# Order of the matmuls inside a contraction step of gate and up: four of 512 columns, then four of 256

## The reference, cut to what matters

```python
def swiglu_ffn(h, w_gate_up, w_down):
    gate, up = jnp.split(h @ w_gate_up, 2, axis=-1)
    return (jax.nn.silu(gate) * up) @ w_down
...
    for layer in range(DEPTH):
        h = h + 0.5 * swiglu_ffn(rms_norm(h, ffn1_norm[layer]), ffn1_w_gate_up[layer], ffn1_w_down[layer])
        ...
        h = h + 0.5 * swiglu_ffn(rms_norm(h, ffn2_norm[layer]), ffn2_w_gate_up[layer], ffn2_w_down[layer])
    return rms_norm(h, final_norm)
```

## Time and profile before

| what | value |
|---|---|
| median of 3 runs | 1030.55 us |
| the runs | 1030.55, 1028.49, 1701.71 us |
| the profiled execution, its own time | 1029.14 us |
| its span, first to last instruction | 1027.4 us |
| TensorE busy | 1016.9 us (99%), 5790 matmuls |
| loads of its stationary operand | 881.5 us (86%), 5790 |
| VectorE busy | 675.4 us (66%) |
| ScalarE busy | 569.1 us (55%) |
| granted TensorE clock, mean | 0.999 |

### The profile page before, as it was taken

The page is one execution under the profiler, slowest core; times in us unless marked ns, Lnnn a source line. Parts: engine busy times, 40 slices in busy tenths (PEclk is TensorE's granted clock), DMA queues, the critical chain, the costliest instruction groups (busy, mean ns, idle before and its releaser), DMA issues.

```text
span 1027.4 us, 15453 instructions
## 1 busy us (share of the span) xinstructions
PE 1016.9 (99%) x5790; PEld 881.5 (86%) x5790; DVE 675.4 (66%) x1005; ACT 569.1 (55%) x907; POOL 60.3 (6%) x120
## 2 busy tenths in 40 slices
PE   8999999999999999999999999999999999999997
PEld 7888888887888888888888888999999988888886
DVE  5766765576566776635766764688597666776733
ACT  7645543457565654536545543577567655554532
POOL 0000000110000000000000000404205100000000
PEclk9999999999999999999999999999999999999999
DMA  9666465343346555563665465343242347556521
GB/s 322 214 208 200 163 245 201 138 165 109 99 130 228 172 186 216 212 199 102 196 213 191 166 243 205 118 155 123 83 144 83 124 144 231 179 176 219 213 87 41
DMA packets 124308, 175.81 MB, mean 171 GB/s; under 512 B 7360, under 2 KB 97760, under 8 KB 124256
## 3 DMA queue, kind: packets, MB, share of 16 engines
q1 hardware_dynamic: 121552, 172.77, 49.5%
q10 hardware_dynamic: 2704, 2.33, 0.7%
HBM read 174.02 MB, written 1.06 MB: 170 GB/s over the span
## 4 chain that ended last, share of the span: by engine, by line
PE 97%; DVE 1%; ACT 1%; DMA 1%; issue 0%; SPq 0%; ACTq 0%; DVEq 0%
PE bank L1761 29%; PE bank L1691 15%; PE bank L1693 15%; PE bank L1692 14%; PE bank L1763 14%; PE bank L2085 2%; PE bank L2079 2%; PE bank L1988 1%; PE bank L1712 1%; PE bank L1923 1%; PE bank L1954 1%; PE bank L1853 1%; DMA w_raw<-in_ffn_w_gate_up 1%; DVE x_sb L1184 0%; PE bank L2182 0%
## 5 line engine op out<-in xcount | busy, mean ns | idle before, releaser
L1761 PE MATMUL bank<-xT,w_hi 128*128 128x512 f32 x1280 | 444.9, 394 | 0.0
L1147 DVE TENSOR_TENSOR w_lo<-w_raw,w_hi 128x2048 fp32r<-128x2048 f32 x152 | 347.4, 2290 | 105.7 <-ACT w_hi L727 105.0
L727 ACT ACTIVATE w_hi<-w_raw 128x2048 fp32r<-128x2048 f32 x153 | 294.0, 1930 | 118.0 <-PE bank L1693 118.0
L1763 PE MATMUL bank<-xT,w_lo 128*128 128x256 f32 x1280 | 354.8, 277 | 0.0
L1761 PEld LDWEIGHTS bank<-xT,w_hi 128*128 128x128 f32 x1280 | 240.0, 188 | 55.7
L1763 PEld LDWEIGHTS bank<-xT,w_lo 128*128 128x128 f32 x1280 | 240.4, 188 | 0.1
L1691 PE MATMUL bank<-w_hi,hT_hi 128*128 128x512 f32 x352 | 137.5, 391 | 0.0
L1693 PE MATMUL bank<-w_hi,hT_lo 128*128 128x512 f32 x352 | 137.0, 389 | 0.0
L1692 PE MATMUL bank<-w_lo,hT_hi 128*128 128x512 f32 x352 | 137.0, 389 | 0.0
L793 ACT ACTIVATE silu_g<-bank 128x256 f32<-128x256 f32 x80 | 26.4, 382 | 175.4 <-PE bank L1763 175.4
L1234 DVE TENSOR_TENSOR silu_g<-bank,silu_g 128x256 f32<-128x256 f32 x80 | 30.2, 419 | 119.5 <-ACT silu_g L793 119.5
(11 more groups left out here) (312 smaller groups left out, 1218.7 us busy)
## 6 DMA issues: line engine op xcount, KB each, us to landing
w_raw<-in_ffn_w_gate_up SPq DMA_DIRECT2D x170, 512.0 KB, 4.6
w_raw<-in_ffn_w_down SPq DMA_DIRECT2D x88, 512.0 KB, 4.0
w_raw<-in_gdn_w_in SPq DMA_DIRECT2D x32, 512.0 KB, 4.4
w_raw<-in_attn_w_in SPq DMA_DIRECT2D x12, 512.0 KB, 4.1
w_raw<-in_attn_w_out SPq DMA_DIRECT2D x8, 512.0 KB, 3.7
w_raw<-in_gdn_w_out SPq DMA_DIRECT2D x8, 512.0 KB, 3.6
w_raw<-in_ffn_w_gate_up SPq DMA_DIRECT2D x12, 256.0 KB, 6.1
x_sb<-in_x SPq DMA_DIRECT2D x4, 256.0 KB, 5.4
```

The source lines that it names most:

```text
L727: act.activation(w_hi[u0 % RING][:], w_raw[u0 % RING][:], ACT.Copy).then_inc(hi_ready, 1)
L1147: dve.tensor_tensor(w_lo[u0 % RING][:], w_raw[u0 % RING][:], w_hi[u0 % RING][:].bitcast(F32), ALU.subtract).then_inc(split_ready, 1)
L1761: pe.matmul(banks[m][:], w[0], xT[:, kt, :, :].rearrange("p s n -> p (s n)"), start=(kt == 0), stop=False, skip_group_check=True)
L1763: z = pe.matmul(banks[m][:, SEQ:2 * SEQ], w[1], xT_hi[:, kt, :], start=False, stop=(kt == KT - 1), skip_group_check=True)
```

## The change

Within a contraction step all four matmuls of line 1761 are issued first, banks 0 to 3, and then the four with `w_lo`, banks 0 to 3. The number of matmuls and of loads, their operands, the waits and the place of `unit_done` (behind the last matmul of a unit, with `w_lo` on bank 3) stay. Each bank still gets its `w_hi` matmul before its `w_lo` matmul of the step. The second kind stands at line 1765 of the new file.

```diff
@@ -1760,6 +1760,8 @@
                             w = ring(u0, slice(q * BANK + m * P, q * BANK + (m + 1) * P))
                             pe.matmul(banks[m][:], w[0], xT[:, kt, :, :].rearrange("p s n -> p (s n)"),
                                       start=(kt == 0), stop=False, skip_group_check=True)
+                        for m in range(4):
+                            w = ring(u0, slice(q * BANK + m * P, q * BANK + (m + 1) * P))
                             z = pe.matmul(banks[m][:, SEQ:2 * SEQ], w[1], xT_hi[:, kt, :], start=False,
                                           stop=(kt == KT - 1), skip_group_check=True)
                     z.then_inc(unit_done, 1)
```

## The result

| | before | after |
|---|---|---|
| median | 1028.61 us (six runs, the three shown above among them) | 1033.32 us (six runs, 1032.77 to 1033.53) |
| ratio | 1 | 1.0042, 95% interval 1.0029 to 1.0055 |
| span of the profiled execution | 1027.4 us | 1031.6 us |

The changed kernel is slower by 4.7 us (1033.32 - 1028.61). That is within the 2% that the forecast called no change, and inside the range given, but it is clear of the scatter of the runs, and the forecast was no difference. The range reached up to 1034 only because the scatter of three runs had been added to a difference of 0.4 us at most. The difference itself lies far outside that. (One of the six runs before, 1701.71 us, stands far off the others and is not in the ratio.)

The account below looks back on a forecast made before the run. TensorE's matmul stream was taken as the bound; 226.7 + 119.9 ns equalled the mixed pair's 346.6 ns, all other terms 0, so 0.0 +- 0.4 us and an unchanged median of 1030.5 us. Range 1027 to 1034 us.

Parts of the forecast that it names:

- What bounds the kernel: Whole kernel: TensorE's matmul stream, busy 1016.9 of 1027.4 us; only its pitch or a wait put into it counts.
- a sum of pitches: Gate and up: each matmul pays its columns plus 13.3 ns whatever stands ahead; 226.7 + 119.9 = 346.6 ns, difference 0.0.
- settled runs of 73 and 154 matmuls: Price sources: 73 starts of 512s in the down projection, 226.7 ns; 154 of 256s in DeltaNet's channel units, 119.9 ns.
- The error bar of 0.4 us: Gate and up's reordered transitions: starts shown to 10 ns leave 960 x 0.4 ns = 0.4 us either way.
- 512 behind 512 and 256 behind 256: The new transitions in gate and up, 960 of each: 226.7 ns and 119.9 ns, priced from other stages.
- The load stays hidden: Stationary loads beside 256s in gate and up: load pitch 111 ns, 9 ns below a 256's 120 ns; cost 0.
- Repeated operand, changing bank: 0: Gate and up: rereading the same moving operand or changing bank at each matmul neither costs nor saves; 0.
- Traffic, waits and releases: 0: Around gate and up: SBUF and DMA contention adds nothing beyond the prices; waits and `unit_done` releases stay; 0.
- The slow one: Rival in gate and up: 188 ns loads hold 960 of the 256s, 65 us more, 1096 us; 3 in 100.
- The fast one: Rival in gate and up: repeated moving operands save 13.3 ns each, 25.5 us, 1005 us; 3 in 100.
- The signs in the profile: Gate and up: chunks 11.09 us apart, line 1761 about 390 ns, `w_lo` about 282, load idle partly moved.
- three signs of being wrong: Gate and up: `w_lo` matmuls beyond 121 ns apart, 512s closer than 226 ns, or TensorE idle ahead of either line.

Follow-up runs that it names:

- short loads: Kernel before with 64 of 128 stationary columns in looped chunks: alternating 10.881 us from chunk to chunk, fours 10.987 us, sixteens 10.986 us.
- two kernels that share little else: The changed kernel, and the kernel before reordered to four 512s then four 256s per bank: 11.226 us from chunk to chunk in both.
- runs of sixteen: Kernel before with a unit's sixteen 512s issued first, then its sixteen 256s: 11.133 us from chunk to chunk, 1029.52 us beside 1028.47.
- runs of four within one bank: Kernel before with, for each bank in turn, a unit's four 512s and then its four 256s: 11.226 us from chunk to chunk, 1033.49 us.
- strict alternation with other banks: Kernel before, but in each chunk's second unit the 256 goes to the next bank: 11.093 us from chunk to chunk, 1028.51 us beside 1028.78.
- one run with the same order: Kernel before's order with 64 stationary columns in looped chunks only; the full-load chunk behind the transposes took 11.30 us, 11.09 us before.

## Why the prediction was wrong, point by point

**What bounds the kernel: right.** All of the difference is TensorE's pitch in gate and up, and the other engines only follow.

**The step that failed** is the sentence that a sum of pitches "doesn't depend on the order". From 226.7 + 119.9 = 346.6 ns being equal to the measured mixed pair, I took it that each matmul pays its own price whoever stands ahead of it. The equality is real but it belongs to one pattern: the other pattern lies 6.7 ns above the sum, and with short loads the alternation lies 3.3 ns below it (340.0 against 343.3). The kernel before held the counterexample: the first unit of the same loop at 353 ns a pair, 20 us ahead of the stretch that I read. With two pitches for one alternation no sum of single prices can be right, and prices from settled runs of 73 and 154 matmuls say nothing of runs of four. The error bar of 0.4 us was the rounding of the starts, not the doubt whether the rule carried over. What the runs show in its place is a pitch that depends on the sequence of lengths (11.226 us for a chunk in two kernels that share little else) and, for the alternation, on what went before (346.7 or 353.3 ns a pair). In the changed kernel each step of eight costs 16.7 ns more than the sum; 320 steps make 5.3 us of that; without the first chunk of each feed-forward, where the order before was no faster, it is 288 steps and 4.8 us.

**512 behind 512 and 256 behind 256** as settled pitches held: 228 and 120 ns in runs of sixteen in this very stage.

**The load stays hidden** held in its consequence, since no 256 stands further apart than 120 ns on the mean. As a statement on the mechanism it was too simple: with half the stationary columns both pitches moved, in opposite directions, and the trip between runs became free. The Trainium skill (TensorE: Matmul & The Clock Gate, Part 2: What happens when you issue a matmul) says that loading the next weights takes no read bandwidth from the running matmul. These runs don't measure bandwidth. They show that the pitch depends on the stationary side, 120 to 114 ns for a 256 and 226.7 to 230.0 ns for a 512, but not whether through the load or through the 64 output rows.

**Repeated operand, changing bank: 0** held, shown by the runs of four within one bank (11.226 us with neither) and by the strict alternation with other banks (11.093 us).

**Traffic, waits and releases: 0** held. In the second feed-forward the DMA share of a chunk's window ranges from 0.51 to 0.71 before and from 0.52 to 0.76 after, and every chunk behind the first is 11.09 us long before and 11.23 us after.

**The rivals.** The slow one named the right sign and a wrong mechanism and size (65 us). The fast one didn't occur. What was missing was a rival by which a run of four differs from both a settled run and an alternation; its bound could have been had from the heads of the long runs (the 512s that follow gate and up from 410.11 us in the kernel before start 231, 224, 231, 235, 229, 232, 231 and then 227 ns apart in the trace) and from the slow first unit: 6.7 ns for each of 1280 pairs is 8.5 us to the slow side.

**The signs in the profile.** The mean length of the `w_lo` line came as forecast (277 to 281 ns). That of line 1761 went the other way, from 394 to 395 ns where 390 was given, the first hint that its pitch had not settled. The idle time of the load path was split, 29.6 and 27.3 us. The chunks were to stay 11.09 us apart and are 11.23. But none of the three signs of being wrong came true in its mean: they asked for 256s beyond 121 ns, 512s closer than 226 ns, or idle time, and the 512s stood 232 ns apart. The signs did not watch the side on which the sum failed.

**What stays open.** Which part of TensorE makes the patterns. Neither banks, nor operands, nor waits do; the sequence of moving lengths and the number of stationary columns both enter. Why runs of four settle where they do, and what decides between the two patterns of an alternation, is open too. No run here looks inside.

## What to carry to other kernels

Where a stream of matmuls is the bound, read its pitch over whole periods and in every stretch of the loop, the first one too: a second pitch for the same instructions says that prices can't be added up, and that even a reorder of equal work can cost. Take the price of a new sequence from a stretch with the same run lengths, or doubt the sum by as much as the two pitches differ. A strict alternation of long and short can run at the speed of the settled sum, but one irregular step may put all that follows into a slower pattern, so look behind it and not only at it.

## What the runs showed of the hardware that was not expected

- One alternation of 512 and 256 columns has two steady patterns, 346.7 and 353.3 ns a pair at clock 1.00. Four matmuls in another order moved it from the first to the second for 90 us. Behind six transposes of 128 columns it changed as well, from the second to the first in the kernel before and from the first to the second in one run with the same order.
- A return trip between runs costs 3.3 ns for runs of two, 16.7 for four, 20 for eight and for sixteen. The pitches of the alternations (340.0 with 64 stationary columns, 346.7, 353.3) lie 6.67 ns apart, which is as long as 16 periods of 2.4 GHz; no run shows a reason for it.
- With 64 stationary columns in place of 128, a 256 went from 120 to some 114 ns and a 512 from 226.7 up to a mean of 230.0 ns, and a trip between runs of four cost no more than one between runs of sixteen.
